# Two transformer layers in one kernel: cross-attention copies moved ahead of sums and splits, a second output bank for the first attention, and four smaller moves of order

## What is computed

```python
def first_block(x, ...):
    h = rms_norm(x, norm_mix_g)
    (g_qkv, g_z, g_a, g_b, a_q, a_k, a_v, i_q, i_k, i_w, gate_a, gate_b) = split(h @ w_in)
    qkv = silu(causal_short_conv(g_qkv, conv_w))        # 4 taps, 3072 channels
    o_gdn = gated_delta_rule_chunked(l2(gq), l2(gk), gv, g, beta)
    o_gdn = rms_norm(o_gdn) * silu(g_z)
    o_att = dsa_sparse_attention(a_q, a_k, a_v, i_q, i_k, i_w)   # index scores choose 64 keys
    x = x + (sigmoid(gate_a) * o_gdn + sigmoid(gate_b) * o_att) @ w_out
    return x + square(relu(rms_norm(x) @ w_mlp_up)) @ w_mlp_down

def second_block(x, mem, ...):
    # retention and forgetting attention side by side, 8 heads of 64 each
    h = x + concat([silu(rg) * norm(ret), fox]) @ w_out
    h = h + memory_cross_attention(rmsnorm(h), mem, ...)     # 4 heads of 256, 256 memories
    return h + (silu(hn @ w_gate) * (hn @ w_up)) @ w_down
```

## Time and profile before

| | us |
|---|---|
| median of 3 executions | 910.66 |
| lowest and highest | 910.09, 911.07 |
| the profiled execution | 910.86 |
| its span in the profile | 909.1 |
| PE busy in the span | 895.3 |
| DVE busy | 589.5 |
| ACT busy | 448.1 |
| POOL busy | 113.0 |

### The profile page before, as it was taken

How to read it: one execution, slowest core, us unless ns; L and a number is a source line. 1 busy time by engine, 2 the same in 40 slices (tenths; PEclk the granted TensorE clock), 3 DMA queues, 4 the chain that set the end, 5 groups by cost and what they waited for, 6 DMA issues and landing times.

```text
span 909.1 us, 12635 instructions
## 1 busy us (share of the span) xinstructions
PE 895.3 (98%) x5039; PEld 764.6 (84%) x5039; DVE 589.5 (65%) x849; ACT 448.1 (49%) x631; POOL 113.0 (12%) x84
## 2 busy tenths in 40 slices
PE   9999999999999999999999999999989999999998
PEld 6887887888978999988888889888878888889886
DVE  5378988996796566654455747977776565554542
ACT  6265456854535555533344336646544544444431
POOL 0431225665110000000000002100100000000200
PEclk9999999999999999999999999999999999999999
DMA  8774542344235555555567635524532565554562
GB/s 284 200 252 140 185 139 85 127 127 114 93 103 176 184 180 179 185 193 187 186 194 280 196 94 186 185 94 139 171 107 86 167 203 186 185 169 152 188 215 70
DMA packets 83555, 149.74 MB, mean 165 GB/s; under 512 B 8481, under 2 KB 16209, under 8 KB 83377
## 3 DMA queue, kind: packets, MB, share of 16 engines
q1 hardware_dynamic: 80352, 144.55, 49.0%
q10 hardware_dynamic: 2528, 3.63, 1.1%
q0 software_dynamic: 624, 0.87, 0.8%
HBM read 147.59 MB, written 1.44 MB: 164 GB/s over the span
## 4 chain that ended last, share of the span: by engine, by line
PE 84%; DVE 9%; ACT 3%; DMA 2%; POOL 1%; issue 1%; SPq 0%; ACTq 0%; POOLq 0%; DVEq 0%
PE gemm L495 61%; PE mixbank L979 5%; PE gemm L979 5%; DMA raw<-in_w_in_dram 2%; DVE w_lo L1810 2%; DVE mix L2039 2%; PE mixbank L556 1%; PE mixbank L678 1%; PE mixbank L653 1%; ACT w_hi L1258 1%; PE mixbank L1151 1%; PE mixbank L840 1%; PE gemm L567 1%; PE gemm L1179 1%; PE mixbank L664 1%
## 5 line engine op out<-in xcount | busy, mean ns | idle before, releaser
L1810 DVE TENSOR_TENSOR w_lo<-raw,w_hi 128x2048 fp32r<-128x2048 f32 (+3 forms) x131 | 284.9, 2184 | 189.9 <-ACT w_hi L1258 189.4
L1258 ACT ACTIVATE w_hi<-raw 128x2048 fp32r<-128x2048 f32 (+3 forms) x140 | 255.4, 1832 | 177.3 <-DMA raw<-in_w_in_dram 52.0
L495 PE MATMUL gemm<-w_hi,s_hi 128*128 128x512 f32 (+3 forms) x784 | 209.1, 387 | 1.0 <-issue 0.6
L495 PE MATMUL gemm<-w_lo,s_hi 128*128 128x512 f32 (+3 forms) x784 | 201.8, 377 | 0.1
L495 PE MATMUL gemm<-w_hi,s_lo 128*128 128x512 f32 (+3 forms) x784 | 201.7, 377 | 0.0
L495 PEld LDWEIGHTS gemm<-w_lo,s_hi 128*128 128x128 f32 x784 | 142.7, 188 | 27.7 <-DVE w_lo L1810 0.3
L495 PEld LDWEIGHTS gemm<-w_hi,s_lo 128*128 128x128 f32 x784 | 142.7, 188 | 27.5
L495 PEld LDWEIGHTS gemm<-w_hi,s_hi 128*128 128x128 f32 x784 | 139.5, 188 | 27.6 <-issue 2.8
L2616 POOL TENSOR_TENSOR sm<-sm 128x2 f32<-128x2 f32 (+5 forms) x13 | 22.0, 1695 | 460.5 <-DVE sm L1854 303.2
L2610 POOL TENSOR_TENSOR w_lo<-raw,w_hi 128x2048 fp32r<-128x2048 f32 x9 | 41.3, 4598 | 158.2 <-ACT w_hi L1258 158.2
L1275 ACT ACTIVATE mix<-gemm,sm 128x512 f32<-128x512 f32 (+2 forms) x25 | 16.3, 653 | 56.1 <-PE gemm L495 56.1
(11 more groups left out here) (348 smaller groups left out, 1167.5 us busy)
## 6 DMA issues: line engine op xcount, KB each, us to landing
raw<-in_w_in_dram SPq DMA_DIRECT2D x40, 1024.0 KB, 5.1
raw<-in_w_mlp_up_dram SPq DMA_DIRECT2D x16, 1024.0 KB, 5.6
raw<-in_w_mlp_down_dram SPq DMA_DIRECT2D x16, 1024.0 KB, 5.1
raw<-in_w_gate_dram SPq DMA_DIRECT2D x10, 1024.0 KB, 5.1
raw<-in_w_up_dram SPq DMA_DIRECT2D x10, 1024.0 KB, 5.1
raw<-in_w_down_dram SPq DMA_DIRECT2D x10, 1024.0 KB, 5.1
raw<-in_w_out_dram SPq DMA_DIRECT2D x8, 1024.0 KB, 5.0
raw<-in_w_xkv_dram SPq DMA_DIRECT2D x8, 1024.0 KB, 5.1
```

The costliest lines, as they stand in the source:

```text
L495: return nc.tensor.matmul(G[b % 2][t][:, 0:width], lhs, rhs, start=kt == 0 and not (low_x or low_w), stop=kt == blk["kt"] - 1 and (low_x i ...
L1258: nc.scalar.activation(w_hi[:, n % SLOTS, 0:kn, 0:width], raw[:, n % SLOTS, 0:kn, 0:width], ACT.Copy)\
L1810: V.tensor_tensor(w_lo[:, s, 0:kn, 0:width], raw[:, s, 0:kn, 0:width], w_hi[:, s, 0:kn, 0:width].bitcast(F32), ALU.subtract)\
```

## The change

Six edits. (1) PE makes two idle products instead of three and none behind the turns; ACT splits only the first 128 rows of the first half chunk and DVE the second 128 rows, and PE waits for both. (2) The first quarter of `B_Q + 1` goes ahead of the index turns. (3) `attention` takes a list of output banks; the first attention gets two, `G[1][0]` and `M[3]`, the second keeps `M[3]`. At `k == n` the weighing goes ahead of the turn. The first two turns of the convolution are issued at the last two steps of the first attention. (4) ACT's exponentials `EG` and `ED` go behind the second first tap. (5) `taps` waits for each half of two taps by itself. (6) In the cross attention the copies of operands go ahead of squares and splits on ACT and DVE.

```diff
+        ATT_OUT = [G[B_GB % 2][0], M[3]]
...
                         if b == 0:
                             pe.wait_ge(sem("split_hi" if pair % 2 else "first_hi"), c + 1)
+                            if pair == 0:
+                                pe.wait_ge(sem("vec_dve"), 2)
...
-            spin(3)
+            spin(2)
...
             turn(xtile, lambda q: [(f"x_in{q}", 16)], banks=range(2))
-            spin(1)
             mm(B_A, turned=4, quarters=[0])
...
+            mm(B_Q + 1, quarters=[0])
             pe.wait_ge(sem("idx_rot"), 1)
             operands(range(3))
-            mm(B_Q + 1)
+            mm(B_Q + 1, quarters=[1, 2, 3])
...
-                    if k >= 1:
-
-                        pe.wait_ge(sem("att_norm"), g)
+                    if k >= len(outs):
+
+                        pe.wait_ge(sem("att_norm"), g - len(outs) + 1)
...
                     yield k
+                    if k == n:
+                        weighed(k - 2)
                     if 1 <= k <= n:
                         turned(k - 1)
-                    if k >= 2:
+                    if k >= 2 and k != n:
                         weighed(k - 2)
...
                 if 1 <= k <= 4:
                     mm(B_Q + 5, quarters=[k - 1])
+                if k == 2:
+
+                    pe.wait_ge(sem("ev0"), B_Q + 5)
+                    pe.wait_ge(sem("ev1"), B_Q + 5)
+                if k >= 6:
+                    pe.wait_ge(sem("att_exp"), k - 1)
+                    turned_in(k - 6)
...
-            turned_in(0)
-            turned_in(1)
+            pe.wait_ge(sem("att_norm"), 5)
             fill(0)
...
-            act.wait_ge(sem("gdn_gcc"), 2)
-            nc.scalar.activation(EG, GC[:, 0:16], ACT.Exp)
-            nc.scalar.activation(ED, GC[:, 16:32], ACT.Exp).then_inc(sem("gdn_e"), 1)
...
             first_tap(1)
+            act.wait_ge(sem("gdn_gcc"), 2)
+            nc.scalar.activation(EG, GC[:, 0:16], ACT.Exp)
+            nc.scalar.activation(ED, GC[:, 16:32], ACT.Exp).then_inc(sem("gdn_e"), 1)
             conv_tanh(0)
...
-            query_sums(0)
             cross_operand(0)
             cross_operand(2)
+            query_sums(0)
+            cross_operand(4)
             split(B_XO, 0)
-            cross_operand(4)
...
+            dve.wait_ge(sem("first0"), 16)
+            V.tensor_copy(w_hi[:, 0, 1, :], raw[:, 0, 1, :]).then_inc(sem("vec_dve"), 1)
...
                         y = YT[:, ct, tap:SEQ]
+                        if tap > 1:
+
+                            dve.wait_ge(sem("dve_step"), seen["dve_step"] - (0 if tap == 3 and j == 1 else 1))
                         ins = V.scalar_tensor_tensor(...)
-                    if tap < 3:
-                        link(ins)
+                        if tap < 3:
+                            sig(ins, "dve_step")
...
-            query_means(0)
             cross_operand(1)
             cross_operand(3)
-            split(B_XO, 0)
+            query_means(0)
             cross_operand(5)
             query_scales(0)
+            split(B_XO, 0)
+            cross_max(0)
             split(B_XO, 1)
-            cross_max(0)
```

More of the change, by code:

```diff
@@ L635, in _, with attention @@
             groups = [0]
-            def attention(work, queries, keys, values, width, exps, exps_turned):
+            def attention(work, queries, keys, values, width, exps, exps_turned, outs):
                 g0, n = groups[0], len(work)
@@ L677, in weighed @@
                         for s in range(per):
-                            last = nc.tensor.matmul(M[3][:, j * width:(j + 1) * width], exps_turned[:, g % 2, (j * per + s) * P:][:, 0:P],
+                            last = nc.tensor.matmul(outs[k % len(outs)][:, j * width:(j + 1) * width], exps_turned[:, g % 2, (j * per + s) * P:][:, 0:P],
                                                     values(h, s), start=s == 0, stop=s == per - 1)
@@ L685, in attention @@
                     yield k
+                    if k == n:
+                        weighed(k - 2)
                     if 1 <= k <= n:
                         turned(k - 1)
-                    if k >= 2:
+                    if k >= 2 and k != n:
                         weighed(k - 2)
                 groups[0] += n
[L693 to L698, removed]
-            pe.wait_ge(sem("att_ptc"), 6)
-            pe.wait_ge(sem("ev0"), B_Q + 6)
-            pe.wait_ge(sem("ev1"), B_Q + 6)
-            pe.wait_ge(sem("gdn_g"), 1)
-            nc.tensor.matmul(M[2][:, 0:16], cst[:, C_CUM:C_CUM + P], GA_, start=True, stop=True)
-            nc.tensor.matmul(M[2][:, 16:32], cst[:, C_ONES:C_ONES + P], GA_, start=True, stop=True).then_inc(sem("gdn_gc"), 1)
             def turned_in(s):
@@ L717, in turned_in @@
                 last.then_inc(sem("conv_pe"), 1)
+            pe.wait_ge(sem("relu"), 6)
+            for k in attention(WORK_A, lambda h: [qT[:, h, :]], lambda h: [kT[:, h // 4, :]],
+                               lambda h, s: PA[:, s, AV + P * (h // 4):AV + P * (h // 4) + P], P,
+                               LM, PTS, ATT_OUT):
+                if 1 <= k <= 4:
+                    mm(B_Q + 5, quarters=[k - 1])
+                if k == 2:
[4 more added lines that the diff above has]
+                    turned_in(k - 6)
+            pe.wait_ge(sem("att_ptc"), 6)
+            pe.wait_ge(sem("ev0"), B_Q + 6)
+            pe.wait_ge(sem("ev1"), B_Q + 6)
+            pe.wait_ge(sem("gdn_g"), 1)
+            nc.tensor.matmul(M[2][:, 0:16], cst[:, C_CUM:C_CUM + P], GA_, start=True, stop=True)
+            nc.tensor.matmul(M[2][:, 16:32], cst[:, C_ONES:C_ONES + P], GA_, start=True, stop=True).then_inc(sem("gdn_gc"), 1)
             def turned_back(i):
@@ L1098, in _ @@
             for k in attention(WORK_A, lambda h: [qaT[0:66, h, :]], lambda h: [kaT[0:66, h, :]],
-                               lambda h, s: P2F[:, s, FV - 2048 + 64 * h:FV - 2048 + 64 * h + 64], 64, LM2, PTS2):
+                               lambda h, s: P2F[:, s, FV - 2048 + 64 * h:FV - 2048 + 64 * h + 64], 64, LM2, PTS2, M[3:4]):
                 if k == 0:
@@ L1304, in _ @@
                 act.wait_ge(sem(f"loaded{c}" if j else f"first{c}"), 16)
-                nc.scalar.activation(w_hi[:, c, 2 * j:2 * j + 2, :], raw[:, c, 2 * j:2 * j + 2, :], ACT.Copy)\
+                k = slice(0, 1) if q == 0 else slice(2 * j, 2 * j + 2)
+                nc.scalar.activation(w_hi[:, c, k, :], raw[:, c, k, :], ACT.Copy)\
                     .then_inc(sem("split_hi" if j else "first_hi"), 1)
@@ L1872, in _ @@
                 dve.wait_ge(sem("split_hi" if j else "first_hi"), c + 1)
+                if q == 0:
+                    dve.wait_ge(sem("vec_dve"), 2)
                 V.tensor_tensor(w_lo[:, c, k, :], raw[:, c, k, :], w_hi[:, c, k, :].bitcast(F32), ALU.subtract)\
@@ L1971, in _, with attention @@
             groups = [0]
-            def attention(work, scale, width, mask, lm, pts, dst):
+            def attention(work, scale, width, mask, lm, pts, dst, outs):
                 g0, n = groups[0], len(work)
@@ L2009, in normed @@
                     dve.wait_ge(sem("att_out"), g + 1)
-                    V.tensor_tensor(dst(t, hs), M[3][:, 0:width * len(hs)].rearrange("p (a b) -> p a b", b=width),
+                    V.tensor_tensor(dst(t, hs), outs[k % len(outs)][:, 0:width * len(hs)].rearrange("p (a b) -> p a b", b=width),
                                     spread(RSUM[:, a:a + len(hs)], 2, width), ALU.mult).then_inc(sem("att_norm"), 1)
@@ L2021, in attention @@
                 groups[0] += n
-            for k in attention(WORK_A, P ** -0.5, P, lambda t: BIAS[:, t, 0:P * (t + 1)], LM, PTS, lambda t, hs: OA[:, t, hs[0]:hs[-1] + 1, :]):
+            for k in attention(WORK_A, P ** -0.5, P, lambda t: BIAS[:, t, 0:P * (t + 1)], LM, PTS, lambda t, hs: OA[:, t, hs[0]:hs[-1] + 1, :], ATT_OUT):
                 if k == 1:
@@ L2409, in _ @@
             for k in attention(WORK_A, 1.0, 64, fox_mask, LM2, PTS2,
-                               lambda t, hs: MG2[:, t, NCOL + 64 * hs[0]:NCOL + 64 * hs[-1] + 64].rearrange("p (a b) -> p a b", b=64)):
+                               lambda t, hs: MG2[:, t, NCOL + 64 * hs[0]:NCOL + 64 * hs[-1] + 64].rearrange("p (a b) -> p a b", b=64), M[3:4]):
                 if k in (1, 3):
```

## The result

The changed kernel takes **905.55 us** (median of 5 runs, 905.39 to 906.03), the kernel before on the same chip 910.59: ratio 0.9941, 95% interval 0.9931 to 0.9952. That is 5.0 us less, where 4.2 were forecast. The profiled execution took 905.39, with a span of 903.6.

A forecast was written before the change was run, and what follows sets the result against it. TensorE (PE) was taken as the bound. From 910.86 us, start and index -0.25, first attention -0.4, taps -0.6 and cross attention -2.9 gave 906.7 profiled, 906.5 as median; range 904.9 to 908.5.

The forecast's parts named there:

- Cross attention, -2.9: Cross attention: operand copies ahead of squares and splits remove both PE stops, 1.16 and 1.45 us printed; -2.9 us.
- The slack named for cross_scaled(0): Cross attention: VectorE's scaling, now behind a second w_lo, ends at 674.5, PE asks at 674.9; 0.4 us of slack.
- Taps by halves, -0.6: Convolution: waiting for the half before last saves VectorE 0.22 us in each of 12 groups; -0.6 us reaches PE.
- the bounds: Taps at L749: 0 if the next instruction cannot start earlier, -1.15 us if both PE stops go.
- End of the first attention, -0.4 with a new stop of 0.9 for GU: End of first attention: last weighing starts earlier, but PE then waits 0.9 us for GpSimd's GU product; -0.4 us.
- two output banks are worth nothing: Middle of the first attention: PE does not stop there, so a second output bank gains nothing.
- The start, -0.8: First block: fewer idle products let PE start earlier, capped by the load of x's last quarter; -0.8 us.
- The late-clock rival: First block: the clock rises late with fewer idle products, start worth 0, index move +0.55; 907.3 us, chance 0.20.
- The index move, +0.55: Block B_Q+1: a quarter ahead of index turns delays VectorE, losing PE's 0.5 us gain at first attention; +0.55 us net.
- the sum of 906.7: Whole kernel: 910.86 - 0.25 - 0.4 - 0.6 - 2.9 = 906.7 us for the profiled execution.
- The prediction's own list of signs: Trace signs of being right or wrong, including PE waiting for ScalarE or w_lo near 110 to 124 by about the start's gain.
- the rival in which the index move is harmless: Start and first attention: index move costs nothing, -0.8 - 0.5 replaces -0.25; 905.5 us, chance 0.12.

The follow-up runs named there:

- the experiment: The changed kernel with one output bank (M[3]) instead of two for the first attention: 907.08 us, ratio 0.9965.
- the start alone: The kernel before with only two idle products instead of four and the first weight split shared with VectorE: 910.15 us, ratio 0.9991.
- The repeat: The changed kernel measured once more, with nothing altered: 905.68 us, ratio 0.9947.

## Why the prediction was right, and where it was not

**Cross attention, -2.9: right.** 3.06 between two points of the trace, the same when done alone. The slack named for cross_scaled(0) held: no wait of L1173 appears.

**Taps by halves, -0.6: right**, in pitch (0.26 against 0.22 a group) and in what reaches PE: 0.6 us between the decay rows and the cross attention, 0 with whole waits. One of the two stops went, the other (0.5) stayed, as halfway between the bounds. By the drain rule of the Trainium skill (VectorE: DVE Perf Modes, The DRAIN you can't avoid) this part would have been worth 0; the measurement disagrees, 0.6 us at PE. The same section adds that a next operation that is not held starts earlier, and with that the trace agrees: 0.40 us from start to start for operations of 0.48. The exponentials' move, counted within this term, brought nothing without the waits by halves.

**End of the first attention, -0.4 with a new stop of 0.9 for GU: right in sum**, -0.4 between 124 and the decay rows, and the stop measured 0.72 + 0.16. The step that placed PE's new stop behind GpSimd's GU product held as well: moving a filling quarter into it gave 0.76. But "two output banks are worth nothing" was said of the middle, and I carried it to the end in the experiment's expectation. There the gain needs the second bank: without it the same order costs 0.8 where it gave 0.4.

**The start, -0.8: the mechanism right, the size left to a load.** PE runs at full pace from the first product, and the last quarter of x caps the lead, as predicted; the landing varies, and the lead with it: 1.3 us in one trace, 0.4 in another of the same kernel, 1.0 with the start alone. The late-clock rival fell at two idle products, and shows what it would cost at none.

**The index move, +0.55: this step failed.** It put ScalarE's and VectorE's delay of 1.6 us on PE at the first attention, less 0.97 of idle time. Two things were missed. First, what absorbs it. In the kernel before VectorE's first bias operation is long, and ends with GpSimd's:

```profile
115.63 4.60 POOL L2610 TENSOR_TENSOR w_lo<-raw,w_hi 128x2048 fp32r<-128x2048 f32 x1 [8.51 <-ACT w_hi L1258]
118.94 1.38 DVE L1967 TENSOR_SCALAR mix<-mix 128x128 f32<-128x128 f32 x1
```

In the changed kernel:

```profile
113.45 4.61 POOL L2629 TENSOR_TENSOR w_lo<-raw,w_hi 128x2048 fp32r<-128x2048 f32 x1 [8.63 <-ACT w_hi L1269]
117.54 0.60 DVE L1983 TENSOR_SCALAR mix<-mix 128x128 f32<-128x128 f32 x1
```

VectorE ended this operation with GpSimd's, at 120.3 and 118.1; the 1.15 us beyond the 0.23 that this form takes when GpSimd is not at work (114.06 and 116.61 above) was slack that the page books as busy time. I had read only idle time as slack. With it VectorE reached the attention 2.2 us earlier, and both stops at L664 went. Second, VectorE's lateness showed ahead of the attention: PE stopped for w_lo at 109.07, 1.09 + 0.16, in place of the stops at L602 (0.34 + 0.16) and at the first L664 (0.39 + 0.16). That is 1.25 against 1.05 us: the two nearly balance. Start and index together gave 0.4 to 1.4 where 0.25 was said. In the first trace that is 1.1 of the 1.3 us by which the profiled time, 905.39, lies under the sum of 906.7 (about 0.5 from the start, 0.4 from the stretch in between that nothing was changed in, 0.2 from the index move); the cross attention gave the rest. The prediction's own list of signs had named a wait for w_lo near 110 to 124; its sum had no term for it.

**The number.** 905.55 lies in the stated range, but just under the 905.7 to 907.4 of the case that was forecast, and on the 905.5 of the rival in which the index move is harmless and both the start and the stop at L602 are kept whole. It is partly luck that it falls there: the move gave back about what it took, the stop for w_lo was new, and what the start was worth hung on a load.

**What stays open.** By the starts of the same products, PE's lead over the kernel before changes by -0.2 to +0.6 us between 12 and 60 us, mostly between 46 and 50, from trace to trace (+0.4 and +0.3 in the two of the changed kernel). ScalarE's split at 45.03 in the kernel before had waited 11.1 us for a load of weights, so landing times may be behind it; that was not pursued. The repeat's profiled execution took 906.30 at a median of 905.68, so one trace is good to about half a microsecond.

## What to carry to other kernels

When an engine's operation is longer than its form is elsewhere, look at what the other engines were doing at its end: the excess can be a wait that no list of waits shows, slack for whoever delays that engine and a trap for whoever moves its work under another engine's. When an operation is moved across a queue, follow its wait too: a reorder that frees one stop can need the buffer that lets it run early. Here the order without the second bank was a loss (the bank without the order was not tried). And a lead won ahead of a load is worth what the load leaves of it, which is read from several executions, not one.

## What the runs showed of the hardware

- GpSimd's TENSOR_TENSOR on two operands (4.6 us) holds some operations of VectorE until it ends: TENSOR_SCALAR out of SBUF (0.23 became 1.38, 1.27 and 1.51 on 128x128; 0.17 became 3.52 on 128x4) and TENSOR_TENSOR with both inputs in SBUF (0.29 became 4.61). The custom operations that read a PSUM bank and one other operand (0.28) ran on meanwhile, as did MAX8 (0.62) and MATCH_REPLACE8 (0.28) in the kernel before. The Trainium skill (SBUF — State Buffer, Who interferes with whom) states such a rule, a port pair held for a whole instruction by GpSimd or by a VectorE operation that uses its second port; the trace agrees.
- Dependent VectorE operations of 0.48 us take 2.42 us for six when each waits for the one before last, and 2.68 when a pair waits for a pair.
- PE, which had only waited and made nine short turns, ran its first eight products at the 1.2 GHz level (0.47, then 0.43 us each, against 0.25 and 0.23); with two idle products in that time, none.
